# Feed-forward of tokens 0 to 255 moved beside the expert gather, up- and down-projection fused by chunks; every pick on TensorE

## What is computed

```python
# first block, expert layer, per token t and pick k
act = gelu(einsum('td,tkd->tk', xt, peer_u[it]))
y   = einsum('tk,tkd->td', gt * act, peer_v[it])
# second block, feed-forward (D_FF = 2816), over all tokens
u = causal_conv3(norm(h) @ w_up) + conv_b
h = h + gate * ((silu(u[:half]) * u[half:]) @ w_down)
```

## Time and profile before

| what | value |
|---|---|
| median of 3 executions | 2609.31 us (2605.87 to 2611.97) |
| the profiled execution, first to last instruction | 2607.3 us |
| busy: TensorE, VectorE, ScalarE, GpSimd | 2152.8, 1647.3, 1003.4, 702.4 us |
| moved | 683.18 MB, of them 536.90 MB by the indirect transfers |
| gather, first dot product to last product | 673.6 to 2033.7 us |
| feed-forward, first to last matmul | 2230.5 to 2599.3 us |

### The profile page before, as it was taken

How to read it: one execution, slowest core, us unless ns; L and a number is a source line. 1 busy time by engine, 2 the same in 40 slices (tenths; PEclk the granted TensorE clock), 3 DMA queues, 4 the chain that set the end, 5 groups by cost and what they waited for, 6 DMA issues and landing times. The chain is left out here.

```text
span 2607.3 us, 25567 instructions
## 1 busy us (share of the span) xinstructions
PE 2152.8 (83%) x8090; PEld 1334.7 (51%) x8090; DVE 1647.3 (63%) x3381; ACT 1003.4 (38%) x2477; POOL 702.4 (27%) x610
## 2 busy tenths in 40 slices
PE   6999978897878687877868887676777787899998
PEld 6778855676423232322324453232333474788877
DVE  5674266535888988878456776656766555555534
ACT  3213345323443343333334344435533455433322
POOL 0120031000444354443434454444444100000000
PEclk8999988998999899898989999787988897999999
DMA  7664200211899999999999999999999433222222
GB/s 243 218 208 113 67 5 26 77 61 75 340 419 420 400 403 420 396 420 398 415 380 415 414 414 411 420 370 359 420 419 420 159 92 122 91 97 97 80 81 97
DMA packets 142827, 683.18 MB, mean 262 GB/s; under 512 B 19648, under 2 KB 36320, under 8 KB 74224
## 3 DMA queue, kind: packets, MB, share of 16 engines
q0 software_dynamic: 73728, 536.90, 50.3%
q1 hardware_dynamic: 68976, 144.78, 17.0%
HBM read 679.50 MB, written 2.10 MB: 261 GB/s over the span
## 5 line engine op out<-in xcount | busy, mean ns | idle before, releaser
L2483 PE MATMUL peer_Y<-peer_w,peer_diag 128*128 128x512 f32 x1784 | 902.5, 645 | 242.2 <-ACT peer_diag L2469 215.2
L2428 POOL DMA_INDIRECT peer_w<-in_peer_uv,peer_eidx x510 | 606.4, 1189 | 703.7 <-PE peer_Y L2483 465.8
L2437 DVE CUSTOM_DVE_ANT_0 peer_w<-peer_w,peer_xtok 128x1024 f32<-128x1024 f32 x510 | 617.7, 1222 | 198.1 <-DMA peer_w<-in_peer_uv,peer_eidx 195.3
L2483 PEld LDWEIGHTS peer_Y<-peer_w,peer_diag 128*128 128x128 f32 x1784 | 337.8, 202 | 753.2 <-ACT peer_diag L2469 443.7
L2461 ACT ACTIVATE peer_gel<-peer_dots 128x1 f32<-128x1 f32 x512 | 103.8, 203 | 721.8 <-DVE peer_dots L2437 721.5
L2469 ACT ACTIVATE peer_diag<-all_ident,peer_a 128x128 f32<-128x128 f32 x448 | 179.8, 401 | 18.1 <-PE peer_Y L2483 3.6
L2463 ACT ACTIVATE peer_a<-peer_gel,peer_gates 128x1 f32<-128x1 f32 x512 | 150.8, 294 | 16.6
L2992 PE MATMUL m_acc<-m2x_hs,m2x_cut 128*128 128x512 f32 (+1 forms) x384 | 143.7, 374 | 6.4 <-PEq L123 3.7
L2993 PE MATMUL m_acc<-m2x_hs,m2x_cut 128*128 128x512 f32 (+1 forms) x384 | 143.3, 373 | 0.0
L2994 PE MATMUL m_acc<-m2x_hs,m2x_cut 128*128 128x512 f32 (+1 forms) x384 | 143.2, 373 | 0.0
L1293 ACT ACTIVATE p_cut<-m1h_raw 128x512 fp32r<-128x512 f32 (+2 forms) x96 | 58.2, 609 | 202.1 <-PE p_acc L1240 119.3
(11 more groups left out here) (518 smaller groups left out, 3731.2 us busy)
## 6 DMA issues: line engine op xcount, KB each, us to landing
m_gates<-in_w_ada SPq DMA_DIRECT2D x48, 512.0 KB, 4.3
m2x_raw<-in_w_up SPq DMA_DIRECT2D x22, 1024.0 KB, 4.8
m1h_raw<-in_w_in SPq DMA_DIRECT2D x80, 256.0 KB, 3.1
m20h_raw<-in_w_in SPq DMA_DIRECT2D x48, 256.0 KB, 7.3
m22h_raw<-in_w_in SPq DMA_DIRECT2D x48, 256.0 KB, 2.8
m_down_ring<-in_w_down SPq DMA_DIRECT2D x22, 512.0 KB, 3.4
m_out_ring<-in_w_out SPq DMA_DIRECT2D x16, 512.0 KB, 7.8
peer_w<-in_peer_uv,peer_eidx POOLq DMA_INDIRECT x510, 16.7
```

Of the source, the lines that this page charges most:

```text
L2428: pool.indirect_dma_start(self.slot(n).rearrange("p c n -> p (c n)"), None, self.uv_dram, bass.IndirectOffsetOnAxis(self.col(self.eidx, n) ...
L2437: dve.tensor_tensor_reduce(u, u, self.xtok[:, n // PICKS, :], 1.0, 0.0, ALU.mult, ALU.add, self.col(self.dots, n)).then_inc(self.dotted, 1)
L2483: ins = pe.matmul(self.Y[:, h, :], self.diag[:, i % self.RD, :], self.slot(n)[:, 1, h * BANK:(h + 1) * BANK], start=(k == 0), stop=(i == l ...
```

## The change

- The feed-forward works on two tiles at a time (`second_ffn` and `ffn_half`). For tiles 0 and 1 (names `f0...`) it runs while the gather still goes on, after `second_front` of these tiles and before `finish_gather`; for tiles 2 and 3 (`f2...`) at the end, alone. Every weight of it is loaded and split twice.
- Up- and down-product are fused: the work is a line of 100 units. Units 0 to 87 are quarters of the 22 chunks (one half, four of the eight row blocks: 12 matmuls of 256 columns); the convolution of a chunk, its Silu, the product of the halves, the splits for the down-product and the down-product itself (12 matmuls of 512 columns) follow at fixed distances of 5 to 12 units. `gT` is gone.
- The last two columns of each chunk of tiles 0 and 1 are kept (`kept.before`) for the convolution of tile 2.
- The gather's guests are shared out anew: 8, 56, 30, 32 and 28 steps beside the front part, 6 beside the new norm, 88 beside `ffn_half`, the last 8 in `finish_gather`.
- `FOLDED` is gone: all 512 picks are spread on a diagonal and added by TensorE. The class has code for pairs of picks on half diagonals, which is never reached: `PAIRED = 4`, and `single(n)` holds for every n below 4 * 128.
- Between the front part and the feed-forward of tiles 0 and 1 stands a barrier of all engines and a recycling of semaphores. `UpAhead`, `Opening`, `out_closing`, `ffn_up` are removed; the ring of weight pieces in the front part has 5 slots in place of 6.

```diff
 class Gather:
-    FOLDED = range(2 * PICKS, NT * PICKS)
-    SHARE = 4
+    PAIRED = 4
...
+    def single(self, n):
+        return n < self.PAIRED * PICKS
...
-        act.activation(self.col(self.gel, n), self.col(self.dots, n), ACT.Gelu).then_inc(self.gelued, 1)
+        act.activation(self.col(self.a, n), self.col(self.dots, n), ACT.Gelu).then_inc(self.gelued, 1)
...
 def peer_and_front(nc, consts, resid, mod, d, kept, stats):
...
+        second_front(nc, consts, resid, mod, d, kept, HALF, xtok[:, 0:2, :], inputs, pacer)
+        gather.fetch_to(nc.gpsimd, pacer.next)
+        nc.multi_engine_barrier(Straight.ALL)
+        Phase.recycle(nc)
+        second_ffn(nc, consts, resid, mod, d, kept, None, HALF, pacer, xtok[:, 0:2, :], inputs)
         finish_gather(nc, gather, pacer.next)
...
+def ffn_half(nc, name, consts, resid, d, kept, group, hs, cut, ring, u, conv, before, side=ALONE, out_dram=None):
+    IDENT, TAPS, SILU, MULT, SPLIT, DOWN = 5, 6, 7, 8, 10, 12
...
+        @block.scalar
+        def _(act):
+            for v in ENDS:
+                if v < UNITS:
...
+                    if v >= CUT:
+                        act.wait_ge(used, v - CUT + 1)
+                    act.activation(cut[v % CUT][:, 0], raw[v % RAW], ACT.Copy).then_inc(hi_made, 1)
+                c = chunk(v, SPLIT)
+                if c is not None:
...
+                    act.activation(wcut[:, 0, :], down[c % RD], ACT.Copy).then_inc(w_hi, 1)
+                    act.wait_ge(multed, c + 1)
+                    act.activation(acut[:, 0, :], u[:, c % 2, 1, :], ACT.Copy).then_inc(a_hi, 1)
+                c = chunk(v, IDENT)
...
+                        ins = act.activation(u[:, c % 2, g, :], up(c)[:, g, :], ACT.Identity, bias=cb[:, 2 * c + g:2 * c + g + 1], scale=tap(c, g, 2))
...
+                c = chunk(v, SILU)
+                if c is not None:
+                    act.wait_ge(conved, c + 1)
+                    act.activation(u[:, c % 2, 0, :], u[:, c % 2, 0, :], ACT.Silu).then_inc(silued, 1)
+                side.scalar(act, v)
...
+        @block.tensor
+        def _(pe):
+            for v in ENDS:
+                if v < UNITS:
...
+                    for j in range(4):
+                        k = k0 + j
+                        pe.matmul(up(c)[:, g, :], hi[:, j, :], hs[:, 0, k, :], start=(k == 0), stop=False)
+                        pe.matmul(up(c)[:, g, :], hi[:, j, :], hs[:, 1, k, :], start=False, stop=False)
+                        ins = pe.matmul(up(c)[:, g, :], lo[:, j, :], hs[:, 0, k, :], start=False, stop=(k == KD - 1))
+                    ins.then_inc(used, 1)
+                c = chunk(v, DOWN)
...
+                side.tensor(pe, v)
...
+        @block.vector
+        def _(dve):
+            for v in ENDS:
+                if v < UNITS:
+                    dve.wait_ge(hi_made, v + 1)
+                    dve.tensor_tensor(cut[v % CUT][:, 1], raw[v % RAW], cut[v % CUT][:, 0].bitcast(F32), ALU.subtract).then_inc(lo_made, 1)
...
+                side.vector(dve, v)
...
-                    beside = side(85, len(jobs) * KD)
+                    beside = side(56, len(jobs) * KD)
...
+        ffn_half(nc, name + "m", consts, resid, d, kept, group, hs, cut, ring, u, conv, None if hosted else kept.before, side(88, 4 * NF + 12), None if hosted else out)
```

More of the change, by code:

```diff
@@ L303 @@
 ALONE = Alone()
[L306 to L352, removed]
@@ L517, in norm_transpose @@
[L517 removed]
+def norm_transpose(nc, name, consts, resid, hs, gain_dram, meta=None, mod=None, load=None, tokens=range(NT), early=(), keep=None, side=ALONE, first_col=0, whole=None):
     ident, half = consts["ident"], consts["half"]
@@ L2474, in tensor @@
+        n = s - 2
+        if n % 2 or not 0 <= n < self.N or self.single(n):
             return
         t, k = divmod(n, PICKS)
-        i = self.products(n)
-        pe.wait_ge(self.diaged, i + 1)
-        pe.wait_ge(*self.landing(n))
-        if k == 0 and t >= 1:
+        pe.wait_ge(self.spread, n + 2)
+        if k == 0:
             pe.wait_ge(self.added, 2 * t)
-        last = self.products((t + 1) * PICKS) - 1
-        for h in range(2):
-            ins = pe.matmul(self.Y[:, h, :], self.diag[:, i % self.RD, :], self.slot(n)[:, 1, h * BANK:(h + 1) * BANK],
-                            start=(k == 0), stop=(i == last))
@@ L2485, in tensor @@
-        ins.then_inc(self.used, 1)
-def pick(nc, gather, top, qT, keys, mod, rows, steps):
-    ident = gather.consts["ident"]
+        for j in range(2):
+            pe.wait_ge(*self.landing(n + j))
+        for turn in range(2):
+            if turn == 0:
+                pe.wait_ge(self.used, self.products(n))
+            else:
+                pe.wait_ge(self.crossed, self.products(n) - self.PAIRED * PICKS + 1)
+            for j in range(2):
+                for r in range(2):
+                    h, half = (r + turn) % 2, (r + j) % 2
+                    rows, out = slice(64 * r, 64 * r + 64), slice(64 * half, 64 * half + 64)
+                    ins = pe.matmul(self.Y[out, h, :], self.stationary(n + j)[rows, :], self.slot(n + j)[rows, 1, h * BANK:(h + 1) * BANK],
+                                    start=(k == 0 and turn == 0), stop=(k == PICKS - 2 and turn == 1))
+            ins.then_inc(self.used if turn else self.crossed, 1)
@@ L2491, in pick @@
+def pick(nc, gather, ident, top, qT, keys, mod, rows, steps):
     FAST, PACES = 112, (3, 2)
@@ new lines, with __init__, up, lower @@
+class Ahead:
+    def __init__(self, d, raw, down, early, early_down):
+        self.raw, self.down, self.early, self.early_down, self.d = raw, down, early, early_down, d
+        self.loads = [(raw[v], self.up(v)) for v in range(early)] + [(down[c], self.lower(c)) for c in range(early_down)]
+    def up(self, v):
+        c, g, half = v // 4, v // 2 % 2, v % 2
+        return self.d["w_up"][c, :, g, 4 * half:4 * half + 4]
+    def lower(self, c):
+        return self.d["w_down"][c * P:(c + 1) * P, :]
@@ new lines, in load_down @@
+            def load_down(c):
+                sp.dma_start(down[c % RD], ring.lower(c)).then_inc(down_landed[c % RD], 16)
+            for v in range(E, RAW):
+                load(v)
+            for c in range(ED, RD):
+                load_down(c)
+            for v in ENDS:
+                if RAW <= v < UNITS:
+                    sp.wait_ge(lo_made, v - RAW + 1)
+                    load(v)
+                c = chunk(v, SPLIT + 1)
+                if c is not None and c + RD < NF:
+                    sp.wait_ge(w_lo, c + 1)
+                    load_down(c + RD)
@@ L3170, in second_ffn @@
[L3170 to L3177 removed]
+        attention(nc, name + "a", consts, at(qT), at(kept.kT), kept.av, None, dilated, 0, DIL_E ** -0.5, mixT[:, 4:8, :], [out_ring],
+                  tiles=group, slots=2 if pacer is not None else 4, side=side(32, DIL_H * n // 2 + 1))
```

542 lines of the change are left out of this document (182 added, 360 removed).

## The result

| | before | after |
|---|---|---|
| median | 2609.91 us (4 runs, 2605.87 to 2611.97) | 2846.28 us (4 runs, 2842.87 to 2849.57) |
| profiled span | 2607.3 us | 2841.1 us |
| feed-forward matmuls of tiles 0 and 1 | | 1877.5 to 2294.1 us |
| last feed-forward, first to last matmul | 2230.5 to 2599.3 us | 2530.6 to 2836 us |

What follows compares the result with a forecast made beforehand. Transfers, the ScalarE-VectorE ring and TensorE were taken to bound different stages. Gather end at 2289 us, late front part 191 and late feed-forward 218 sum to 2698; with 2.0 us, 2700, slower by 3.5%; range 2632 to 2775.

Steps and rivals of the forecast that it cites:

- Hosted feed-forward, 412: Feed-forward of tiles 0 and 1 beside the gather: 385 us for 22 chunks plus 27 for the last 12 units.
- The ring: ScalarE and VectorE wait for each other once a unit; said to bound hosted projection and feed-forward, 17.5 us a chunk.
- 385 for 22 chunks: Hosted feed-forward, units with weight pieces: 22 chunks at 17.5 us each, the longest of three possible bounds.
- The signs named beforehand: Hosted feed-forward: ScalarE waits longest for dot products, VectorE little for transfers, share near 0.7, 44 table loads, chunks 17 to 18 us.
- Table loads: Hosted feed-forward, a chunk's fourth unit: two loads around Silu at 1.28 us each, no drain; 4.4 us against 3.4 without.
- Projection: Projection beside the gather, 85 to 56 steps: 29 picks less at 1.14 us each, 205 us (ends 175 and 238).
- gla to output projection: gla, attention and output projection, 147 to 90 steps: transfers bound, 142 us less, 264 us (ends 249 and 341).
- norms and barrier: Norm before the projection 26 us, barrier and recycling of semaphores 4, norm of the feed-forward 25.
- the folds' removal: VectorE no longer folds picks beside the gather: worth nothing, since ScalarE's work covered the folds.
- Late feed-forward, 218: Tiles 2 and 3 after the gather: norm 18, TensorE-bound chunks 187, ends 5 and 8; 218 us where 375 stood.
- a late feed-forward over 230 us: Feed-forward of tiles 2 and 3: a time above this was named as a sign that the forecast is wrong.
- the half clock in the hosted stage: Rival: TensorE at clock 0.83 stops ScalarE in the hosted feed-forward, up to 72 us more, 2772 us; chance 0.12.

Runs made afterwards that it cites:

- e3: Changed kernel with the down-weight load's wait moved back in the transfer queue and two buffers for late split down weights and activations: 2721.62 us, ratio 1.0423.
- e5: e3 with ScalarE's hi split made one unit ahead in the hosted feed-forward: 2664.15 us, ratio 1.0211.
- e6: e3 with PAIRED = 2, so two picks share one diagonal pass in tiles 2 and 3: 2735.94 us, ratio 1.0486.
- e7: e3 with every fourth pick of tiles 2 and 3 folded by VectorE, as in the kernel before: 2707.09 us, ratio 1.0375.
- e8: e3 with Gelu in place of Silu in the hosted feed-forward, so no table changes there (another function computed): 2700.34 us, ratio 1.0349.
- e11: The kernel before the change, with only ScalarE's split one unit ahead in the projection beside the gather: 2607.79 us, ratio 0.9997.
- e9: e5 with e7's folds and ScalarE's split one unit ahead in the hosted projection too: 2641.99 us, ratio 1.0123.
- e10: e5 with ScalarE's split one unit ahead in the hosted projection and e6's pairs: 2649.94 us, ratio 1.0137.

## Why the prediction was right or wrong

*Direction.* Right, and with both faults mended (e3, 110 us slower) for the reason given: sending half of the products beside the gather costs more there than it gives back later. But 125 of the 236 us are the two faults, which the reason does not cover.

*Hosted feed-forward, 412.* Measured 420. The ring bounded it: e5 removed it and a chunk went from 16.8 to 14.2 us; e6 and e7 gave TensorE room and gained 3 us there at most. But 385 for 22 chunks against 388 measured is partly luck. With the transfer queue mended the ring alone takes 369, 16.8 a chunk; my turns were 0.7 a chunk too long, and the queue's wait, which I had not followed, added the difference. The signs named beforehand were there: 44 table loads, chunks of 17.6 us, ScalarE waiting longest for dot products (147.2 us), VectorE not at all for transfers. The share was 0.79 instead of 0.7: the transfers were busy for 0.79 x 17.6 = 13.9 us a chunk, not 12.5.

*Table loads.* Forecast at 1.28 us each, without the drain. Loads and turn came out so, and what the loads cost in all was 21 us (e8; 18 if each kernel is set against its own measurement of the one before), where I had given 24 as their end.

*Picks taken off the stages before.* Projection 193 for 205, gla to output projection 281 for 264, norms and barrier 68 for 55: 18 us more together; the first two lie inside their ends; the norms had been given none. Part of the excess is the folds' removal, priced at nothing: e7 gained 11 to 15 us by undoing it.

*Late feed-forward, 218: the step that failed.* The text says: "Then TensorE bounds, with no picks" and "ScalarE and VectorE need about 5 and 7 us a chunk against 8.5, and run ahead here." The durations were right (110.85 / 22 = 5.0 and 152.29 / 22 = 6.9 us a chunk), the conclusion was not: here the engines ran ahead only as far as their buffers and the transfer queue's list let them. I compared busy times and looked up neither. `wcut` has one buffer, so ScalarE's down split can't run further ahead than two units (71 us), and SP's list has the down load's wait ahead of pieces that it delays (53 us, hosted part included). Together 125 us; without them the late stage's matmuls take 201 us instead of 305, and the whole 2721.62, against 2700. I had followed the lists of the engines, and not SP's. The forecast had named "a late feed-forward over 230 us" as the sign of error, and it took 329.

*The range.* Its upper end took in the half clock in the hosted stage, which did not come there (0.97); the clock was low in the late stage (0.89), where I had given it no price. No case had a fault in the late stage, so all ends there were missing.

*The kernel before.* "The ring bounds" in its projection was half the truth (e11): the ring and the transfers both lay at 238 us.

## What to carry to other kernels

Busy time per chunk says which engine could bound; whether the others run ahead is told by two more things, the number of buffers of each tile that crosses engines, and what stands behind each wait in every in-order list, the transfer queue's among them. A wait in the list that issues loads belongs where the list would reach it at the time it is met, not one unit behind it. When a lead or another relief gains nothing, see which wait grew in its place before the theory is dropped.

## What was not expected of the hardware

The same busy share moved less in the hosted feed-forward: 361 to 367 GB/s at a share of 0.96 (e5, e9), where picks alone gave 420 at 1.01. Weight pieces of 256 KB between the picks are not the whole reason, as the projection before has them too and moved 413 at 1.02; the cause stays open.

The kernels with pairs on half diagonals had a lower mean granted clock over the span (0.906 in e6 against 0.941 in e3, 0.908 in e10 against 0.939 in e5). Whether the clock or the pairs' own waits cost e6 its 14 us stays open.
